# Rotary, head transposes and log-sigmoid made inside the input projection; gMLP norm beside the recurrent output; modulation slots moved

## What is computed

```python
for l in range(2):
    mod = cond @ w_ada[l] + b_ada[l]               # 6 vectors of 1024
    h = rms_norm(x, g_mix[l]) * (1 + sc1) + sh1
    z = h @ w_in[l]                                # 256 x 2884
    aq, ak, av, iq, ik, iw, bq, bf, bi, bg, cuv = split(z)
    a_out = dsa_mixer(rope(aq), rope(ak), av, rope(iq), rope(ik), iw)  # top 64 keys by index scores
    b_out = hgrn2_mixer(bq, bf, bi, bg, lower_bounds[l], onorm[l])
    c_out = gmlp_mixer(cuv, ...)                   # gelu, layer_norm of v, spatial matmul
    x = x + g1 * (concat(a_out, b_out, c_out) @ w_out[l])
    h = rms_norm(x, g_ffn[l]) * (1 + sc2) + sh2
    x = x + g2 * (swiglu(h) if l == 0 else moe_swiglu(h))
# hgrn2: log_f = logaddexp(log lb, log1p(-lb) + log_sigmoid(f)); kk = -expm1(log_f);
#        chunked recurrence with decays; o = rms_norm(o, onorm) * silu(g)
```

## Time and profile before

| | |
|---|---|
| runs (3) | 2692.20, 2692.26, 2698.76 us |
| the profiled execution's own time | 2694.83 us |
| its span in the profile | 2692.6 us |
| PE busy | 2402.0 us, 89% |
| DVE busy | 1908.0 us, 71% |
| ACT busy | 1360.0 us, 51% |
| mean granted clock | 0.917 |

### The profile page before, as it was taken

The page is one execution under the profiler, slowest core; times in us unless marked ns, Lnnn a source line. Parts: engine busy times, 40 slices in busy tenths (PEclk is TensorE's granted clock), DMA queues, the critical chain, the costliest instruction groups (busy, mean ns, idle before and its releaser), DMA issues.

```text
span 2692.6 us, 30782 instructions
## 1 busy us (share of the span) xinstructions
PE 2402.0 (89%) x12623; PEld 2001.1 (74%) x12623; DVE 1908.0 (71%) x2287; ACT 1360.0 (51%) x1342; POOL 28.5 (1%) x53
## 2 busy tenths in 40 slices
PE   6987899898667999999999999996947998978998
PEld 4746799774556888888888888884836997745998
DVE  5666644656464888888888888886454888665787
ACT  5233333522323777777777776774334433365342
POOL 1000000000000000000000000000000000000000
PEclk9987899998676999999999999998967999868999
DMA  9552455745016999999999999995502554412453
GB/s 345 160 184 67 134 187 188 274 155 189 16 44 197 356 355 353 354 356 356 354 355 353 358 353 355 342 362 192 173 16 88 175 186 158 136 40 72 147 184 108
DMA packets 293750, 590.71 MB, mean 219 GB/s; under 512 B 11718, under 2 KB 86580, under 8 KB 292960
## 3 DMA queue, kind: packets, MB, share of 16 engines
q1 hardware_dynamic: 289872, 572.33, 60.5%
q0 software_dynamic: 3728, 16.32, 2.0%
HBM read 587.56 MB, written 1.05 MB: 219 GB/s over the span
## 4 chain that ended last, share of the span: by engine, by line
PE 61%; DVE 4%; ACT 2%; DMA 1%; issue 1%; DVEq 0%; SPq 0%; ACTq 0%
PE ps L1162 18%; PE ps L1164 18%; PE ps L1163 18%; PE ps L1257 1%; PE ps L1381 1%; PE ps L1364 1%; PE ps L1242 1%; PE ps L1342 1%; ACT arena L909 1%; DVE arena L1905 1%; PE ps L1280 1%; DVE arena L1703 1%; DVE xT_lo L1735 0%; DVE w_lo L1688 0%; PE ps L1231 0%
## 5 line engine op out<-in xcount | busy, mean ns | idle before, releaser
L809 ACT ACTIVATE w_hi<-raw 128x2048 fp32r<-128x2048 f32 x524 | 994.9, 1906 | 541.2 <-PE ps L1164 421.8
L1688 DVE TENSOR_TENSOR w_lo<-raw,w_hi 128x2048 fp32r<-128x2048 f32 x524 | 1171.3, 2272 | 51.1 <-ACT w_hi L809 48.6
L1162 PE MATMUL ps<-w_hi,xT_hi 128*128 128x512 f32 (+4 forms) x1504 | 602.9, 401 | 54.6 <-DVE xT_lo L1735 20.0
L1163 PE MATMUL ps<-w_lo,xT_hi 128*128 128x512 f32 (+4 forms) x1504 | 589.2, 392 | 0.0
L1164 PE MATMUL ps<-w_hi,xT_lo 128*128 128x512 f32 (+4 forms) x1504 | 589.0, 392 | 0.0
L1162 PEld LDWEIGHTS ps<-w_hi,xT_hi 128*128 128x128 f32 x1504 | 291.6, 194 | 120.0 <-DVE xT_lo L1735 22.2
L1163 PEld LDWEIGHTS ps<-w_lo,xT_hi 128*128 128x128 f32 x1504 | 291.7, 194 | 58.4 <-issue 3.4
L1164 PEld LDWEIGHTS ps<-w_hi,xT_lo 128*128 128x128 f32 x1504 | 291.3, 194 | 58.9
L1162 PE MATMUL ps<-xT_hi,w_hi 128*128 128x256 f32 x1056 | 302.0, 286 | 6.0 <-DVE xT_lo L1735 6.0
L1163 PE MATMUL ps<-xT_lo,w_hi 128*128 128x256 f32 x1056 | 301.5, 285 | 0.0
L1164 PE MATMUL ps<-xT_hi,w_lo 128*128 128x256 f32 x1056 | 301.4, 285 | 0.0
(11 more groups left out here) (333 smaller groups left out, 2049.8 us busy)
## 6 DMA issues: line engine op xcount, KB each, us to landing
raw<-in_moe_w_gate SPq DMA_DIRECT2D x112, 1024.0 KB, 5.4
raw<-in_moe_w_up SPq DMA_DIRECT2D x112, 1024.0 KB, 5.4
raw<-in_moe_w_down SPq DMA_DIRECT2D x112, 1024.0 KB, 5.6
raw<-in_w_ada SPq DMA_DIRECT2D x48, 1024.0 KB, 5.2
raw<-in_f_w_up SPq DMA_DIRECT2D x44, 1024.0 KB, 5.1
raw<-in_f_w_down SPq DMA_DIRECT2D x22, 1024.0 KB, 5.0
raw<-in_w_in SPq DMA_DIRECT2D x20, 1024.0 KB, 5.1
raw<-in_a_w_in SPq DMA_DIRECT2D x12, 1024.0 KB, 5.1
```

Source lines behind the costliest of these rows:

```text
L809: act.activation(w_hi[:, k % HI, 0:LEN[k]], raw[:, r, 0:LEN[k]], ACT.Copy).then_inc(w_hi_ready, 1)
L1162: pe.matmul(out_, lh, rh, start=start, stop=False)
L1163: pe.matmul(out_, lh, rl, start=False, stop=False)
L1688: dve.tensor_tensor(w_lo[:, k % RAW, 0:LEN[k]], raw[:, k % RAW, 0:LEN[k]], w_hi[:, k % HI, 0:LEN[k]].bitcast(F32), ALU.subtract).then_inc( ...
```

## The change

- **Column groups.** In the input projection, VectorE's calls between groups become: group 0 the angles (layer 0), group 1 the rotary of the first 128 tokens (and, in layer 1, the first steps on the lower bounds), group 2 the rotary of the other 128 tokens and the doubled keys, group 3 the absolute value for the log-sigmoid (after the bounds' last steps), group 4 the rest of the log-sigmoid. TensorE transposes the heads between groups 4 and 5, now into banks 4 to 7. ScalarE does its parts between slots.
- **Log-sigmoid.** Its "add 1" on VectorE is dropped: ScalarE gives 1 as the bias of the logarithm.
- **After the projection.** The index scores follow at once, then `whole` slots 0 to 7 in one piece, into banks 0 to 3; ScalarE applies Silu and Gelu to their columns in place there. Slots 8 and 9 come after the recurrent output, 10 and 11 after the output projection, and these two are loaded after `out{l}`, not before.
- **gMLP.** VectorE normalises v and masks the spatial weights before it waits for the recurrent output. The overlapped preparation of the output projection's first slots in `inv_root` goes; ScalarE prepares two slots before the columns, VectorE none before them.
- **Boundary.** The conditioning columns for layer 1 are made at the end of `ffn0`; the angles and sines of the second transformer move into `ffn0` (groups 3 and 4). The bias of `ada10` is loaded to the late place. The bias for `mod[:, 2]` is added after `to_columns`.

```diff
-        WHOLE_BANKS = [4, 5, 6, 7, 4, 4]
+        WHOLE_BANKS = [0, 1, 2, 3, 4, 7]
@@ tensor, in the loop over layers
-                linear(f"in{l}")
...
-                whole(l, range(0, 3))
-                pe.wait_ge(heads_ready, got(heads_ready))
...
+                linear(f"in{l}", between={4: head_columns})
                 pe.wait_ge(heads_sb, got(heads_sb, 4))
...
-                whole(l, range(3, 8))
+                pe.wait_ge(lin_evac, got(lin_evac, 0))
+                pe.wait_ge(cond_wide_ready, l + 1)
+                whole(l, range(0, 8))
...
-                whole(l, range(8, 10))
                 pe.wait_ge(rec_rows, got(rec_rows))
...
-                whole(l, range(10, 12))
+                whole(l, range(8, 10))
                 pe.wait_ge(ws_masked, got(ws_masked))
...
                 linear(f"out{l}")
-                got(ada_sums)
+                whole(l, range(10, 12))
+                got(ada_sums, 2)
                 to_columns(H)
@@ scalar, in the loop over layers
+                upto(base + 11)
+                log_of_sigmoid(h_t1)
+                if l:
+                    act.activation(h_t3[:, 0, :], h_lb[:, 1, :], ACT.Exp).then_inc(lb_comp, 1)
+                act.activation(h_kk, z[:, :, BF:BF + BD], ACT.Sigmoid, scale=-1.0).then_inc(kk_ready, 1)
+                linear(f"in{l}")
+                if l:
+                    log_of_sigmoid(h_t1)
+                copy_heads(headsT..., [(4, 512), (5, 512), (6, 512), (7, 256)], P)
...
-                upto(BASE[f"out{l}"])
-                act.wait_ge(o_out, got(o_out))
-                act.activation(h_sg, z[:, :, BG:BG + BD], ACT.Silu).then_inc(gate_silu, 1)
...
+                root(stat_b[:, 0:2])
                 act.wait_ge(ws_tr, got(ws_tr))
...
+                root(stat_a[:, 0:12])
+                whole_sums(l, [4])
                 upto(BASE[f"out{l}"] + 1)
                 to_columns(3)
                 linear(f"out{l}")
                 norm()
+                whole_sums(l, [5])
@@ vector, in the loop over layers
+                hooks = {1: roped_first, 2: heads_made, 3: forget_begun, 4: forget_made}
+                if l == 0:
+                    hooks[0] = first_angles
+                linear(f"in{l}", into_rows(zrows(IN_DIM)), hooks)
...
-                inv_root(stat_a[:, 0:12], stat_a[:, 0:12], HD, lambda: upto(BASE[f"out{l}"]))
+                inv_root(stat_a[:, 0:12], stat_a[:, 0:12], HD)
...
                 gain_taken()
+                to_columns()
                 dve.wait_ge(ada_sums, 6 * l + 6)
-                tt(mod[:, 2, :], gate_sums[:, :], bias_late[:, 2 * D:3 * D], ALU.add)
-                to_columns()
+                dve.tensor_tensor(mod[:, 2, :], gate_sums[:, :], bias_late[:, 2 * D:3 * D], ALU.add).then_inc(bias_taken, 1)
```

More of the change, by code:

```diff
@@ L608, in build @@
         N_GROUPS = F_DENSE // DG
-        ORDER = ["ada00", "in0", "ada01", "out0", "ffn0", "ada10", "in1", "ada11", "out1", "over", "moe",
+        ORDER = ["ada00", "in0", "ada01", "out0", "gate0", "ffn0", "ada10", "in1", "ada11", "out1", "gate1", "over", "moe",
                  "fa_in", "fa_out", "conv0", "kv", "nsa_in", "kc", "vc", "nsa_out", "conv1"]
@@ L742, in ada_bias @@
                 if half == 0:
-                    pool.wait_ge(mod_free, got(mod_free))
-                load(bias_late if half else arena[:, 0:3 * D], a["b_ada"][l, half * 3 * D:(half + 1) * 3 * D].partition_broadcast(P),
+                    pool.wait_ge(bias_taken, got(bias_taken))
+                else:
+                    pool.wait_ge(bias_free, got(bias_free))
+                load(bias_late, a["b_ada"][l, half * 3 * D:(half + 1) * 3 * D].partition_broadcast(P),
                      ld_mod)
@@ L968, in dense @@
                     act.activation(act_g[:, h:h + 512], gate, ACT.Silu).then_inc(silu_done, 1)
+                    if name == "ffn0" and g == 4:
+                        second_sines()
                     if g >= 2:
@@ L974, in dense @@
                                    ACT.Copy).then_inc(act_hi, 1)
+                if name == "ffn0":
+                    cond_columns()
                 upto(BASE[name] + 3 * N_GROUPS - 1 + HI - 1)
@@ L1091, in _ @@
             linear("fa_in")
[L1092 to L1096, removed]
+            log_of_sigmoid(stat_b)
             root(stat_a[:, 0:16], 4)
@@ L1988, in dense @@
                         dve.wait_ge(w_used, k + 2)
+                    if name == "ffn0" and g == 3:
+                        second_angles()
                     dve.wait_ge(silu_done, got(silu_done))
@@ L2092, in _, with roped @@
             for l in range(2):
+                if l == 0:
+                    condition()
                 ada(f"ada{l}0")
+                if l:
+                    beat().then_inc(lb_free, 1)
+                    dve.wait_ge(lb_free, sent(lb_free))
                 z = zrows(IN_DIM)
-                linear(f"in{l}", into_rows(zrows(IN_DIM)), {} if l else {1: first_angles, 3: second_angles})
-                if l == 0:
-                    dve.wait_ge(sines, got(sines, 2))
-                for b in range(TB):
+                F = z[:, :, BF:BF + BD]
+                def roped(b):
                     for c0, nh in ((AQ, 7), (IQ, 5)):
@@ L2102, in _, with roped_first @@
                              cos1[:, b, :], sin1[:, b, :], rope_t)
-                for i, col in enumerate((AK, IK)):
-                    step(dve.tensor_copy(k_twice[:, i], twice(z[:, :, col:col + HD], [P, TB, 2, HD])))
-                dve.tensor_scalar(iw_half, z[:, :, IW:IW + IDX_HEADS], IDX_HEADS ** -0.5, None, ALU.mult).then_inc(heads_ready, 1)
-                dve.wait_ge(heads_ready, sent(heads_ready))
+                def roped_first():
+                    if l == 0:
+                        dve.wait_ge(sines, got(sines, 2))
+                    roped(0)
+                    if l:
+                        dve.wait_ge(ld_lb, 16)
+                        tt(h_t3[:, 0, :], lb_rows[:, 0, :], lb_rows[:, 1, :], ALU.max)
+                        for k in range(2):
+                            tt(lb_rows[:, k, :], lb_rows[:, k, :], h_t3[:, 0, :], ALU.subtract)
+                        beat().then_inc(lb_diff, 1)
+                        dve.wait_ge(lb_diff, sent(lb_diff))
@@ new lines, in heads_made @@
+                def heads_made():
+                    roped(1)
+                    for i, col in enumerate((AK, IK)):
+                        step(dve.tensor_copy(k_twice[:, i], twice(z[:, :, col:col + HD], [P, TB, 2, HD])))
+                    dve.tensor_scalar(iw_half, z[:, :, IW:IW + IDX_HEADS], IDX_HEADS ** -0.5, None, ALU.mult).then_inc(heads_ready, 1)
+                    dve.wait_ge(heads_ready, sent(heads_ready))
+                    if l:
+                        dve.wait_ge(lb_exp, got(lb_exp))
+                        dve.tensor_tensor(h_t1[:, 0, :], h_t2[:, 0, :], h_t2[:, 1, :], ALU.add).then_inc(lb_sum, 1)
+                        dve.wait_ge(lb_sum, sent(lb_sum))
```

211 lines of the change are left out of this document (99 added, 112 removed).

## The result

The changed kernel takes 2629.8 us (median of 4 runs, 2625.9 to 2632.9) against 2693.4 for the kernel before beside it: ratio 0.976, 95% interval 0.974 to 0.978. Forecast were 2634, with 2617 to 2651 as the range. The profiled execution takes 2629.2 us (span 2627.0) against 2694.8 (span 2692.6): 65.6 us less, where the sum said 58.0.

The account below looks back on a forecast made before the run. Serial steps that leave engines waiting in the first 835 us were taken as the bound. Terms summed to -58.0 us from the profiled 2694.83, giving 2636.8; with the median 2.6 lower, the forecast was 2634 us, range 2617 to 2651.

Parts of the forecast that it names:

- The projection at nothing: Input projection: rotary and log-sigmoid work added on VectorE hides under full TensorE; cost 0, at most 2 x 1.1 us.
- The rival of the lost clock: Both input projections: VectorE overruns idle TensorE in each group, clock stays at 0.50; +100 us, 2734 us; chance 0.03.
- Plain slots as the new bound: Between scores and attention: eight plain slots take 28.1 us, so attention gains 4.9 us in layer 0, 2.0 in layer 1.
- The log-sigmoid from the path: Between attention and recurrence: transposes follow the attention at once, 7.1 us less in layer 0, 28.8 in layer 1.
- Parts 2 and 3: From projection to recurrence: earlier attention plus log-sigmoid off the path, together -12.0 us in layer 0, -30.8 in layer 1.
- The tail: Recurrent output to output projection: v's norm moves ahead, a wait for a root appears; -4.9 us layer 0, -5.5 layer 1.
- Part 5: Behind the output projection: bias and first slot of `ffn0` come after the columns; +3.0 us.
- The boundary: From `ffn0` to `ada10`: conditioning made earlier, TensorE starts sooner, VectorE limits the gain; -6.5 us, bounds 0 and 7.9.
- The clock of the recurrences: Recurrences, both layers: layer 0 loses its preceding slots, layer 1 its idle stretch; taken to cancel, +-6.6 us.
- the rival of slow recurrences: Layer 0's recurrence takes layer 1's longer shape, +6.6 us, tails stay slow, +6; 2646 us; chance 0.14.
- The rival of fast recurrences: Layer 1's recurrence takes layer 0's shape, -6.6 us, router keeps full clock, -5.8; 2621 us; chance 0.13.
- part 7: Small things: angles and sines fit under `ffn0`, one log-sigmoid operation less 0.3 us, router after shorter idle 1.0 us.

Follow-up runs that it names:

- the two repeats: The changed kernel run again unaltered, twice, beside its variants and beside the version with three further edits: 2634.2 and 2628.0 us.
- the late log-sigmoid: The changed kernel with log-sigmoids, bounds and key's sigmoid of both layers put back between attention and recurrence: 2657.0 us, ratio 0.986 to the kernel before.

## Why the prediction was right, point by point

- **The projection at nothing: right.** TensorE has no gap in it, though VectorE ran over in groups 1 and 2 of layer 1 as reckoned (11.8 and 11.3 us from one group's copies to the next for the reckoned 11.7 and 11.2); in 32.40 us it had 3.8 to spare. The rival of the lost clock never began: behind the first 10.9 us (0.86 in layer 0, 0.72 in layer 1, where the kernel before had 0.77) the clock is 1.00.
- **Plain slots as the new bound: right.** 6.9 us of wait foretold, 6.97 and 7.55 found; taken almost away they gave 5.16 us. In layer 1 the scores come 4.1 us later than in layer 0 (98.88 against 94.75 us from the projection's start) and not 2.9: 2.7 by TensorE's wait for ScalarE's copies, 1.4 by a slower start of the projection.
- **The log-sigmoid from the path: right.** Parts 2 and 3 together -12.6 and -31.4 for -12.0 and -30.8. Put back, the steps cost 6.5 and 24.6 us. In layer 1 the sum is partly luck: the scores' delay above is made good by an attention of 16.88 us where layer 0 has 18.23, with a granted clock of 0.70 for 0.63.
- **The tail: right in mechanism, small by 0.6 and 0.7 us.** The wait for the root is 6.24 us as foretold. The two slots took 8.86 us (put at 9.2); the spatial product ran at full clock, 2.00 us where the kernel before had 3.64.
- **Part 5: right.** +3.8 for +3.0, between +2.5 and +3.8 by the three executions.
- **The boundary: right.** -6.8 for -6.5; with the conditioning put back, +6.2 to +7.0. TensorE starts `ada10` at once, 7.6 us sooner behind the start of `ffn0`, and gives 0.8 of it back: VectorE is late for two slots (1.98 and 1.35 us), which the clock of the first 8 us (1.00 for 0.68) does not quite make up for.
- **The clock of the recurrences: the term that failed.** I let two effects of 6.6 us cancel. Layer 0 lost 1.2, layer 1 gained 5.4. Of the two reasons I gave, the idle stretch ahead of layer 1 is only part of it: with the stretch put back, layer 1 took 38.65 us, not 41.71. Plain slots at full clock ahead of layer 0 show no effect: put back, they left it at 36.25. The attentions' low clock (0.63 and 0.70) was no warning either: both recurrences of this execution began at 1.00. The 0.67 that the rival of slow recurrences names is the mean of the idle stretch, not of an attention. The rest varies with no cause in the code, as 36.31 and 39.44 in one kernel show, so a single profile can't size this term to better than 3 us. Whether the kernel before would show 41.7 again stays open; it was profiled once. The rival of fast recurrences came near in its first half (-5.4 for -6.6 in this execution, -2.3 in one of the two repeats) and was wrong in its second: the router did not get its clock back (0.50 over 13.7 us) and won 0.1 us, not the 1.0 of part 7.
- **The remaining 2.3 us** (1.0 before `in0`, 1.3 in the rest) lie inside what runs without an edit in these stretches show: 70.70 to 72.62 over the 13 profiles behind the change, and 1847.0 to 1857.7.

So of the 7.6 us between sum and profile, 4.2 are the two recurrences, 2.0 the start and the rest, and 1.4 all other parts together. That the forecast of 2634 is 4 us from the median says little, as runs of one kernel lie further apart; what bears the prediction out are the parts.

## What to carry to other kernels

When serial work is moved under a full engine, ask which other work it used to cover: the gain ends where that becomes the bound (14 us of earlier top-k gave 6.6, in layer 1 10.6 gave 3.3). After each such move read the two engines' queues once more at the new wait. A wait on an instruction that only stands behind another in its queue goes away when the two change places; here, together with a slot prepared in the time won, that gave 3.4 us per layer. And the first slot of the next product can be prepared while the last one of this product is multiplied: 3.7 us. When effects of a few us are compared in a program of 2.6 ms, compare cut by cut, since the whole varies by more.

## What the hardware showed that was not expected

- The recurrence, the same small matmuls everywhere, took one of a few lengths in the 26 instances of the 13 profiles behind the change: 36.2 to 36.4 us in 16, 39.4 in four, 34.7 in two, 33.1 to 33.2 in two, and 36.6 and 38.7 behind the late log-sigmoid. Length and granted clock go together: behind its first 8 us the mean clock is 0.82 (in one 0.88), 0.73, 0.87 and 0.93 in the first four of these. The Trainium skill, "TensorE: Matmul & The Clock Gate", Part 1, says that the count of slow matmuls at a kernel's start differs between runs of one kernel. By the start of the second input projection the trace agrees, for a start within a kernel: 14, 12 and 11 matmul records stand over 0.4 us apart there in the three executions of the changed kernel, and the others 0.23. The recurrences' 36.31 and 39.44 us show as much where the clock falls and comes back in the midst of the work.
- Idle time ahead of it shows in those first 8 us: 0.75 and 0.70 behind the late log-sigmoid, 0.71 in layer 1 of the kernel before, and 1.00 in all others but one (0.78).
- The recurrent output's 18 matmuls of 64 columns (36 records) took 4.2 us in two instances, at a granted clock of 1.00, and 6.5 to 7.7 in the others, at 0.52 to 0.62.
- ScalarE's change of function again shows no drain: three loads of 1.28 us stand in 5.4 us of layer 1, each with its function 0.01 to 0.02 us behind its end.

```profile
577.57 1.28 ACT L1026 ACT_TABLE_LOAD   x1
578.87 0.94 ACT L1026 ACTIVATE arena<-arena,const 128x768 f32<-128x768 f32 x1
579.83 1.28 ACT L1049 ACT_TABLE_LOAD   x1
581.12 0.53 ACT L1049 ACTIVATE arena<-arena 128x384 f32<-128x384 f32 x1
581.66 1.28 ACT L1050 ACT_TABLE_LOAD   x1
582.96 0.85 ACT L1050 ACTIVATE mix<-Z 128x768 f32<-128x768 f32 x1
```
